# A streaming MLP in two passes over its weights, 21 of 32 chunks with their first products in Strassen's form

## What is computed

```python
for i in range(DEPTH):                       # DEPTH = 2
    y = mixer(x)                             # layer 0: gated short convolution, layer 1: trailing means, grouped map
    h = layer_norm(ALPHA * x + y, ...)
    r = jax.nn.relu(h @ mlp_w1[i])           # 1024 -> 4096, the first products
    f = (r * r) @ mlp_w2[i]                  # 4096 -> 1024, the second products
    e = (p[i] @ ple_w[i]) * jax.nn.sigmoid(h @ ple_gate_w[i])
    x = layer_norm(ALPHA * h + f + e, ...)
```

## Time and profile before

| | |
|---|---|
| median of 3 runs | 2116.04 us (2115.59 to 2116.47) |
| span of the profiled execution | 2114.6 us |
| PE / PEld busy | 2104.2 / 2101.3 us (100% / 99%) |
| DVE busy | 1266.8 us (60%) |
| ACT busy | 821.8 us (39%) |
| DMA, mean | 85 GB/s |
| granted TensorE clock, mean | 0.998 |

### The profile page before, as it was taken

How to read it: one execution, slowest core, us unless ns; L and a number is a source line. 1 busy time by engine, 2 the same in 40 slices (tenths; PEclk the granted TensorE clock), 3 DMA queues, 4 the chain that set the end, 5 groups by cost and what they waited for, 6 DMA issues and landing times.

```text
span 2114.6 us, 31847 instructions
## 1 busy us (share of the span) xinstructions
PE 2104.2 (100%) x13214; PEld 2101.3 (99%) x13214; DVE 1266.8 (60%) x1892; ACT 821.8 (39%) x1287; POOL 74.8 (4%) x69
## 2 busy tenths in 40 slices
PE   9999999999999999999999999999999999999998
PEld 9999999999999999999999999999999999999998
DVE  5232357786454444444787877887875355645477
ACT  4222223663423322222544445555443324233345
POOL 0000000000000000000020002000300000000000
PEclk9999999999999999999999999999999999999999
DMA  4010241444122111111112343543222212122233
GB/s 175 30 60 30 69 129 48 130 129 142 63 85 96 51 50 41 40 60 41 60 54 87 100 147 120 168 139 121 62 77 92 69 51 70 51 80 80 64 107 133
DMA packets 54209, 179.68 MB, mean 85 GB/s; under 512 B 8128, under 2 KB 11328, under 8 KB 54080
## 3 DMA queue, kind: packets, MB, share of 16 engines
q1 hardware_dynamic: 51056, 177.15, 25.7%
q10 hardware_dynamic: 3024, 0.70, 0.2%
HBM read 173.36 MB, written 4.46 MB: 84 GB/s over the span
## 4 chain that ended last, share of the span: by engine, by line
PE 99%; DVE 0%; DMA 0%; SPq 0%; issue 0%; ACT 0%; DVEq 0%
PE ps L699 33%; PE ps L700 33%; PE ps L701 33%; DMA x_raw<-x_t 0%; DVE acc L1187 0%; PE ps L760 0%; PE ps L759 0%; PE ps L728 0%; PE ps L734 0%; SPq L641 0%; PE ps L797 0%; PE ps L724 0%; SPq L653 0%; DVE x_lo L1327 0%; SPq L649 0%
## 5 line engine op out<-in xcount | busy, mean ns | idle before, releaser
L699 PE MATMUL ps<-h_hi,w_split 128*128 128x352 f32 x2160 | 696.9, 323 | 0.4 <-DVE acc L1280 0.4
L700 PE MATMUL ps<-h_lo,w_split 128*128 128x352 f32 x2160 | 691.8, 320 | 0.0
L701 PE MATMUL ps<-h_hi,w_split 128*128 128x352 f32 x2160 | 691.6, 320 | 0.0
L699 PE MATMUL ps<-r_hi,w_split 128*128 128x352 f32 x1634 | 526.9, 322 | 0.0
L700 PE MATMUL ps<-r_lo,w_split 128*128 128x352 f32 x1634 | 523.1, 320 | 0.0
L701 PE MATMUL ps<-r_hi,w_split 128*128 128x352 f32 x1634 | 522.8, 320 | 0.0
L1311 DVE TENSOR_TENSOR acc<-acc,ps 128x352 f32<-128x352 f32 (+1 forms) x769 | 372.6, 516 | 125.5 <-PE ps L701 124.8
L616 DVE TENSOR_TENSOR w_split<-w_raw,w_split 128x1024 fp32r<-128x1024 f32 x291 | 356.5, 1247 | 99.2 <-ACT w_split L889 98.9
L699 PEld LDWEIGHTS ps<-h_hi,w_split 128*128 128x128 f32 x2160 | 405.0, 187 | 1.1 <-issue 1.0
L700 PEld LDWEIGHTS ps<-h_lo,w_split 128*128 128x128 f32 x2160 | 405.9, 188 | 0.0
L701 PEld LDWEIGHTS ps<-h_hi,w_split 128*128 128x128 f32 x2160 | 404.8, 187 | 0.0
(11 more groups left out here) (133 smaller groups left out, 1198.5 us busy)
## 6 DMA issues: line engine op xcount, KB each, us to landing
w_raw<-w_stream SPq DMA_DIRECT2D x315, 512.0 KB, 3.5
x_raw<-x_t SPq DMA_DIRECT2D x4, 704.0 KB, 8.7
y_t<-acc SPq DMA_DIRECT2D x4, 704.0 KB, 4.1
w_raw<-p_t SPq DMA_DIRECT2D x6, 352.0 KB, 2.8
y_t<-acc SPq DMA_DIRECT2D x7, 176.0 KB, 2.0
w_raw<-w_stream SPq DMA_DIRECT2D x3, 256.0 KB, 6.1
x_raw<-x_t SPq DMA_DIRECT2D x4, 176.0 KB, 4.5
x_raw<-x_t SPq DMA_DIRECT2D x2, 352.0 KB, 6.8
```

What stands on the lines that cost most here:

```text
L699: pe.matmul(out, wh, mov_h, start=first, stop=False)
L700: pe.matmul(out, wh, mov_l, start=False, stop=False)
L701: return pe.matmul(out, wl, mov_h, start=False, stop=last)
```

## The change

In each layer the weights of the MLP are now gone through twice, once for groups 0 and 1 together and once for group 2 alone. `ALONE` chunks (2, 4) are still visited for each of the groups 0 and 1 by itself, up to `CLASSIC` (3, 8) for both together as before, and the remaining 13 and 8 chunks for both in the Strassen form (Winograd's variant): with the features halved, the groups 0 and 1 as the two halves of tokens and a chunk's two up tiles as the two halves of outputs, the four up tiles are combined from seven products P1 to P7 of 12 matmuls each. P1, P2 and P4 take plain halves of h. The others take sums of halves, formed once per layer (`ssum`). On the weights' side P1 and P2 take the first unit, P6 and P4 unit Z, P7 and P3 unit Y, P5 the half unit T1. Z, Y and T1 are formed by DVE from the two raw units (`weight_sums`, 4 subtractions of 128x512) and then split into high and low like any unit. DVE combines the products in `part_products` by five additions per chunk.

Per chunk the steps are P1, P6, P2, P7, P5, the down part of the previous chunk's group 0, P3, P4, the down part of its group 1. Group 2's pass takes chunks in twos: 24 matmuls and one add per down tile (in layer 1 the last four chunks singly). All six slots now serve all weights. `PLACES` and `REFILL_LATER` are gone: a refill stands where the slot comes free, and `beside` places the side pieces by estimated costs (`COSTS`), letting an engine fall up to `LATE` = 4 us behind.

```diff
-LEAD = (5, 3), (9, 5)
+CLASSIC = (3,8)
+ALONE = (2,4)
+SINGLES = (0, 4)
...
+PROD_ORDER = (1, 6, 2, 7, 5, 3, 4)
...
+LATE = 4
...
+        for c in range(CLASSIC[layer], NCH):
+            chunk = Chunk(e=count["e"], layer=layer, a=count["a"], t=count["t"], t_free=t_free[0])
+            chunk.before = chunk.t
+            count["e"] += 1
+            u0 = stay(("mlp", layer, c, 0), sums=("mlp", layer, c, 1))
+            second = ("second", ("mlp", layer, c, 1))
+            z, y, v = stay(("stay", u0), "Z"), stay(second, "Y"), stay(second, "T1")
+            unit = {1: u0, 2: u0, 6: z, 4: z, 7: y, 3: y, 5: v}
...
+            def prods(which):
+                for i in which:
+                    use(add("prod", n=0, i=i, chunk=chunk), unit[i])
+            prods(PROD_ORDER[:5])
+            run_downs(layer, pending.pop(0))
+            plan[-1].rectify = chunk
+            outs_at[1] = r_used.get(parts[1], 0)
+            prods(PROD_ORDER[5:])
...
+            if pending:
+                run_downs(layer, pending.pop(0))
+            marks.setdefault("late", []).append((here, chunk))
+            count["t"] += 4
+            t_free[0], t_free[1] = ("r_ready", chunk.t + 1), ("r_ready", chunk.t + 3)
+            down = [None]
+            pending += [(0, [parts[0]], chunk.t + 3, (c, down)), (1, [parts[1]], chunk.t + 4, (c, down))]
...
+    def single_visits(layer):
+        n, pending, done = 2, None, 0
+        while done < NCH:
+            size = 2 if done + 2 <= NCH - SINGLES[layer] else 1
+            parts = []
+            for c in range(done, done + size):
+                part, ready = ups(n, up_units(layer, c))
+                parts.append(part)
+                if pending:
+                    downs(*pending[:3], [u for c0 in pending[3] for u in down_units(layer, c0)])
+                    pending = None
+            pending = (n, parts, ready, list(range(done, done + size)))
+            done += size
+        downs(*pending[:3], [u for c0 in pending[3] for u in down_units(layer, c0)])
...
+        PROD_BANKS = (0, 0, 7, 2, 7, 1, 2)
...
+            def product(step):
+                c, i = step.chunk, step.i
+                bank = PROD_BANKS[i - 1]
+                if i == 1:
+                    pe.wait_ge(a_free, c.a)
+                    wait(pe, rectified, 4 * c.e - 3)
+                elif i == 2:
+                    pe.wait_ge(p_copied, c.e + 1)
+                elif i == 3:
+                    pe.wait_ge(h_sums_lo, 4 * c.layer + 4)
+                    pe.wait_ge(combined, 5 * c.e + 3)
+                elif i == 4:
+                    pe.wait_ge(combined, 5 * c.e + 2)
...
+            def split_sum_hi(u, slot, conds, what):
+                act.wait_ge(w_sums, u.sums)
+                for name, value in conds:
+                    wait(act, sems[name], value)
+                act.copy(slot_of(what, slot, 0), cols_of(what, u)).then_inc(w_hi, 1)
...
+            def rectify(c, i, t):
+                act.activation(t, t if i else ps[:, PROD_BANKS[0], 0:TG], ACT.Relu).then_inc(rectified, 1)
+                act.wait_ge(rectified, 4 * c.e + i + 1)
+                act.activation(t, t, ACT.Square).then_inc(t_squared, 1)
+            def square_hi(c, i, t):
+                act.wait_ge(t_squared, c.t + i + 1)
+                part, f, used = c.outs[i]
+                wait(act, b_full, used)
+                act.copy(rpart(rh, part, f), t).then_inc(r_hi_done, 1)
...
+                    c, i = step.chunk, step.i
+                    if i == 1:
+                        act.wait_ge(p_full, 7 * c.e + 1)
+                        wait(act, r_ready, c.before)
+                        wait(act, y_added, c.layer * NG * KD)
+                        act.copy(vv[:, 0, :], ps[:, PROD_BANKS[0], 0:TG]).then_inc(p_copied, 1)
+                    elif i == 2:
+                        act.wait_ge(p_full, 7 * c.e + 3)
+                        act.wait_ge(sems[c.t_free[0]], c.t_free[1])
+                        rectify(c, 0, tt[:, 0, :])
+                        square_hi(c, 0, tt[:, 0, :])
+                    elif i == 3:
+                        square_hi(c, 1, vv[:, 1, :])
+                        act.wait_ge(combined, 5 * c.e + 4)
+                        rectify(c, 2, tt[:, 1, :])
+                        square_hi(c, 2, tt[:, 1, :])
+                    elif i == 4:
+                        act.wait_ge(combined, 5 * c.e + 5)
+                        rectify(c, 3, vv[:, 0, :])
+                        square_hi(c, 3, vv[:, 0, :])
...
+            def rest_of(c, i, t):
+                part, f, _ = c.outs[i]
+                dve.wait_ge(r_hi_done, c.t + i + 1)
+                dve.tensor_tensor(rpart(rl, part, f), t, f32(rpart(rh, part, f)), ALU.subtract).then_inc(r_ready, 1)
+            def weight_sums(u0, u1):
+                h = U // 2
+                b11, b21, b12, b22 = raw[:, u0.q, 0:h], raw[:, u0.q, h:U], raw[:, u1.q, 0:h], raw[:, u1.q, h:U]
+                dve.wait_ge(raw_in[u1.q], u1.use * 16 + 16)
+                done = u1.sums - 4
+                dve.tensor_tensor(t1[:], b12, b11, ALU.subtract).then_inc(w_sums, 1)
+                dve.tensor_tensor(b12, b22, b12, ALU.subtract).then_inc(w_sums, 1)
+                dve.wait_ge(w_sums, done + 1)
+                dve.tensor_tensor(b11, b22, t1[:], ALU.subtract).then_inc(w_sums, 1)
+                dve.wait_ge(w_sums, done + 3)
+                dve.tensor_tensor(b21, b21, b11, ALU.subtract).then_inc(w_sums, 1)
...
+                    c, i = step.chunk, step.i
+                    at, out, base = {6: (1, vv[:, 0, :], vv[:, 0, :]), 7: (2, vv[:, 1, :], vv[:, 0, :]), 5: (3, vv[:, 1, :], vv[:, 1, :]),
+                                     3: (4, tt[:, 1, :], vv[:, 0, :]), 4: (5, vv[:, 0, :], vv[:, 0, :])}.get(i, (0, None, None))
+                    if at:
+                        dve.wait_ge(p_full, 7 * c.e + PROD_ORDER.index(i) + 1)
+                        if i == 6:
+                            dve.wait_ge(p_copied, c.e + 1)
+                        else:
+                            dve.wait_ge(combined, 5 * c.e + at - 1)
+                        dve.tensor_tensor(out, base, ps[:, PROD_BANKS[i - 1], 0:TG], ALU.add).then_inc(combined, 1)
+                    if i == 7:
+                        rest_of(c, 0, tt[:, 0, :])
+                    elif i == 4:
+                        rest_of(c, 1, vv[:, 1, :])
+                        rest_of(c, 2, tt[:, 1, :])
...
-                for u, slot, _ in step.refill:
-                    split_lo(u, slot)
+                if step.late is not None:
+                    rest_of(step.late, 3, vv[:, 0, :])
+                for kind, u, slot, conds, *more in step.refill:
+                    if kind == "load":
+                        split_lo(u, slot)
+                    elif kind == "half":
+                        dve.wait_ge(w_hi, u.s + 1)
+                        dve.tensor_tensor(slot_of(*more, slot, 1), cols_of(*more, u), f32(slot_of(*more, slot, 0)),
+                                          ALU.subtract).then_inc(w_lo, 1)
+                    else:
+                        weight_sums(u, slot)
```

More of the change, by code:

```diff
@@ L83 @@
     before: object
-@dataclass
+    sums: int = 0
+@dataclass(eq=False)
+class Chunk:
+    e: int
+    layer: int
+    a: int
+    t: int
+    before: int = 0
+    t_free: object = None
+    outs: object = None
+@dataclass(eq=False)
+class Stay:
+    name: object
+    what: str = "load"
+    first: object = None
+    last: object = None
+    conds: object = None
+    slot: int = 0
+    sums: object = None
+@dataclass(eq=False)
 class Step:
@@ L107 @@
     r_need: int = 0
+    chunk: object = None
+    chunks: int = 0
+    rectify: object = None
+    late: object = None
     final: bool = False
@@ L177, in give_slots @@
+        conds = []
+        last = stay.last
+        if last.kind == "down":
+            conds = [("b_full", last.b + len(last.blocks))]
+        elif last.kind == "ple":
+            conds = [("b_full", last.b + 1)]
+        elif last.kind == "prod":
+            conds = [("p_full", 7 * last.chunk.e + PROD_ORDER.index(last.i) + 1)]
+        free[slot] = (end + 1 if stay.name[0] == "grp" else end, conds)
+        stay.first.need.append(key)
     for step in plan:
-        step.slots = [x[1] for x in step.units]
+        step.slots = [stay.slot for stay in step.units]
@@ new lines, in next_part, with ups @@
+    def next_part():
+        count["part"] += 1
+        return (count["part"] - 1) % NG
+    def ups(n, units):
+        part = next_part()
+        for mm in range(CHUNK):
+            a, t = count["a"], count["t"]
+            step = add("up", n=n, part=part, mm=mm, a=a, bank=a % 2, t=t, r_used=r_used.get(part, 0), t_free=t_free[a % 2])
+            use(step, units[mm])
+            count["a"], count["t"] = a + 1, t + 1
+            t_free[a % 2] = ("r_ready", t + 1)
+        return part, count["t"]
@@ new lines, in downs, with up_units, down_units @@
```

(19 more changed lines are left out.)

507 lines of the change are left out of this document (334 added, 173 removed), and 9 rows, old and new, of the table REFILL_LATER.

## The result

The changed kernel takes 2318.4 us (median of 4 runs, 2315.8 to 2320.8), the kernel before 2116.2 beside it: 1.096 times as long, 95% interval 1.094 to 1.097. The forecast was 2214 (2170 to 2242): slower, as said, and above the range by 76 us. Two single executions further down, one of number 8 (3454 us at a mean granted clock of 0.556) and one of number 9 (4197 us at 1.0), are left out of the ratios but counted in those two medians; why they were so slow is open.

What follows compares the result with a forecast made beforehand. PE, busy for the whole span, was taken to set the time. Matmuls saved and waits added, -40.0 + 33.6 + 43.2 + 9.8 + 12.7 + 39 = +98 us, against 2114.6 + 1.4 gave 2214 us, range 2170 to 2242.

Steps and rivals of the forecast that it cites:

- The matmuls removed: In 21 Strassen chunks, 12 matmuls fewer each, 252 in all at 0.1587 us: 40.0 us saved.
- Wait A: At the second down step behind P5, PE waits 1.8 us for DVE's adds in 19 chunks: 33.6 us.
- The walk: Step-by-step timing of DVE's and ACT's rows in order, up to the add PE needs; used to size the waits.
- Wait B: At the second down step behind P4, PE waits 2.5 us for DVE's first add in 17 chunks: 43.2 us.
- The ends of the stretches: First and last chunks of each layer's Strassen stretch: waits of 4.9 us twice (9.8) and 6.3 twice (12.7).
- Side pieces: Side rows in front of two-step down parts make the first adds late at twelve places: 39 us, 10 to 50 kept.
- paired down tiles: Group 2's down tiles need 1.9 us each, leaving 7 us of slack for side pieces: no wait counted.
- The clock falls: Rival: PE's pauses bring half the clock, chunks cost 24 us more, up to 2720 us; chance 0.03.
- restarts: PE starting again after some 57 waits: up to 6 us, kept for the range only.
- Loads at nothing: 68 more loads of 512 KB on the DMA queue were costed at nothing.

Runs made afterwards that it cites:

- number 8: The kernel of experiment 6 with side-row limits of 2 to 3.25, more chunks done alone and 16 Strassen chunks instead of 21: 2159.4 us.
- number 9: The kernel of number 8 with side rows kept out of places with long waits, new limits and two gate loads later: 2176.7 us.
- Experiment 1: Changed kernel with the four weight sums and Z's split moved behind the adds of down steps in the 17 middle Strassen chunks: 2280.3 us.
- Experiment 2: Changed kernel with the casts and low parts of Y and T1 moved to the last down step in the 17 middle Strassen chunks: 2255.6 us.
- experiment 6: The kernel of number 3 with two loads later, layer 0's last second-pass chunks singly, one more layer 1 chunk alone, larger LATE: 2207.3 us.
- experiment 5: Changed kernel with its two passes but no Strassen chunk and no sums of halves: 2220.1 us.
- experiment 11: The kernel before the change, with PE held up 28 times between two down steps by GpSimd, mostly for 0.5 to 1.95 us: 2162.4 us.
- experiment 12: The kernel before the change with the 28 pauses of experiment 11 made longer (58 to 142 columns): 2263.3 us.
- number 7: The kernel of experiment 5 with side rows spread by own limits, more layer 1 chunks alone, layer 0's last second-pass chunks singly: 2167.2 us.
- number 3: Changed kernel with the row moves of Experiment 1 and Experiment 2 together: 2224.4 us.

## Why the prediction was wrong in size and right in sign

**The matmuls removed.** Right: 252 fewer, at 0.1587 where the clock is whole.

**Wait A.** Forecast 19 x 1.8 = 33.6. There are 19: 17 of 1.58 to 1.68 and the second chunk of each stretch with 0.4 and 1.0, 29.5 us. The walk was 0.1 long per chunk. Experiment 1 shows the cause.

**Wait B.** Forecast 17 x 2.5 = 43.2; there are 17 of 2.39 to 2.46, 41.3 us. Experiment 2 shows the cause. The chunk takes 33.3 us where the clock holds (696.63 to 729.93, wait B to wait B), forecast 32.9; 34.9 where it falls (661.76 to 696.63).

**The ends of the stretches.** P2's wait for the copy: 4.7 and 4.8, forecast 4.9, and experiment 6 shows that the loads on P3 and P4 were its cause. The last chunks: 3.4, 1.0 and 0.5, twice, for a forecast of 3.5, 1.4, 1.1 and 0.3: 9.8 instead of 12.7. Strassen's waits together are 90.2 us, forecast 99.3.

**Side pieces: the first term that failed.** Forecast 39, "so I keep 10 to 50". What is left of the idle time is 167.5 - 90.2 = 77.3 us, and experiment 5, which has only such waits, comes near it with 68.5. The walk covered down parts alone. It had none of the eight waits of PE for `h_lo` ahead of a norm's mean (8.0 us), nor that of the output stage (3.6), only some of those for ACT's relu behind the affine ops (11.5), and "I count nothing" for the paired down tiles overlooked 2.9 us behind `w_split`. Of the places walked, 6.9 and 5.3 in layer 0's chunks done alone were 6.2 and 3.1 + 1.8, the end of layer 0 was 7.0 for 5.0, and layer 1 had nine waits behind the adds, 28.9 us, for eight of 20.5. Part of the excess is a cost that the walk did not have: rows of DVE that ran beside GpSimd's window sums took longer. Ahead of the wait of 5.4 at 1562.93:

```profile
1553.42 7.59 POOL L1778 TENSOR_TENSOR win<-win 128x762 f32<-128x762 f32 x4 [7.19 <-ACT win L1290]
...
1554.16 3.47 DVE L1601 SCALAR_TENSOR_TENSOR win<-win,acc 128x640 f32<-128x640 f32 x2
1557.66 3.39 DVE L1607 CAST h_hi<-win 128x640 fp32r<-128x640 f32 x2
```

By the shortest rows of the same shapes these four would take 1.1 and 0.7. Counted alike, the rows ahead of the 2.9 at 1130.94, of the 7.0 at the end of layer 0 and of this wait took 4.9, 2.2 and 5.1 us longer, so up to 10 of the 38 us that the term was short. That is an estimate; no run took GpSimd's sums away.

**The clock: the step that failed.** The sum took every matmul at 1.00, and the rival "The clock falls" got 0.03 because "the clock outlived pauses of this size": a wait of 0.86 us and a microsecond of half-busy PE. These are no pauses of this size. In experiment 11 nothing happened behind pauses of up to 1.95 us, in 12 a fall came behind each of the six of 2.8; B's 2.4 lie between, and 8 of the 17 were followed by one. The rival itself was wrong in kind too. It let the clock stay down for good, up to 2720 us; what comes, in every traced execution, is one stretch of 3.4 to 10.2 us at a pause, and then the clock is back. The page's rule, in the Trainium skill "TensorE: Matmul & The Clock Gate", section "A second HAM failure mode: psum-queue depth-cycling", was nearer than I allowed: brief idling between groups of matmuls did make PE swing between its levels, here at 24 of the 35 waits of over 2 us and 1 of the 29 of 1 to 2. With 60 us at most for it and the rest of the 71.9 put down to starting again 83 times (the forecast had "up to 6 us" for restarts; by experiment 11's 0.29 a time they are up to 24), the terms add up: 2212.6 (the forecast's span) - 9.1 + 38.3 + 71.9 = 2313.7.

**Loads at nothing.** Right: no wait of PE names a DMA.

**What stays open.** Whether a placing exists that makes the two passes as free of waits as the kernel before. The best one tried, number 7, has 34 us of idle left without Strassen. The kernel before keeps three token groups beside each set of weights and a table written out by hand; which of these it owes its 10 us to was not separated.

## What to carry to other kernels

Price a wait of the tensor engine by more than its length: short pauses cost 0.29 us each on top (experiment 11), and in the changed kernel about half of the waits of 2 to 3 us and all above brought 3.4 us or more at half the clock as well, so 167 us more without work cost 239. Work that relieves the bound engine by putting rows on the one behind it is paid for where the bound engine next needs that one's answer, not on average: DVE was 64% busy and yet late at 57 places. So put new rows behind the adds that are waited for, before anything else is tuned (two moves of rows gave 94 us); and test a restructuring without its gain first, since half of the loss here was in the two passes.

## What the runs showed of the hardware

- **A pause and the clock:** see experiments 11 and 12. In experiment 12 the fall begins during the longer pauses or up to 1.2 us after PE has started again.
- **More work can be faster:** 425 unused matmuls took 15.6 us off the changed kernel.
- **GpSimd slows VectorE.** In number 3, while GpSimd ran the window sums, rows of DVE that otherwise take 0.5 to 0.9 us took two to four times as long, and PE then waited 3.0 us:

```profile
1058.91 8.36 POOL L1790 TENSOR_TENSOR win<-win 128x732 f32<-128x732 f32 x4 [10.85 <-ACT win L1298]
...
1063.75 1.96 DVE L1598 TENSOR_TENSOR h_lo<-win,h_hi 128x704 fp32r<-128x704 f32 x1
1065.63 2.02 DVE L1686 TENSOR_TENSOR r_lo<-t,r_hi 128x352 fp32r<-128x352 f32 x1
...
1068.71 0.51 DVE L1686 TENSOR_TENSOR r_lo<-t,r_hi 128x352 fp32r<-128x352 f32 x1
```

The same row, `r_lo` of 352 columns, is 2.02 beside it and 0.51 after it. Not every row is slowed: in the changed kernel all 23 adds of down tiles beside GpSimd's additions, which read PSUM (`ps`), kept to 0.52, while 18 of 29 rows beside them that do not read PSUM took over 1.4 times the shortest of their shape. Beside the single columns that GpSimd set in experiment 12 none was slower.
